# Seven tiles of the first projection as three fp32r products, and five buffers for the modulation chunks of the attention calls

## The reference

```python
cos, sin = axial_rope_tables(ROWS)
xc = ctx
for i in range(DEPTH):
    mod_lat = jax.nn.silu(c) @ w_ada[i] + b_ada[i]
    mod_ctx = jax.nn.silu(c_ctx) @ w_ada[i] + b_ada[i]
    ...
    h = modulate(rmsnorm(x, norm_pre_mix[i]), sh1, sc1)
    hc = modulate(rmsnorm(xc, norm_pre_mix[i]), csh1, csc1)
    p = h @ w_in[i]
    q = apply_axial_rope(p[..., :ATTN_WIDTH].reshape(B, S, N_Q_HEADS, HEAD_DIM), cos, sin)
    k = apply_axial_rope(p[..., kv_lo:kv_lo + KV_WIDTH].reshape(B, S, N_KV_HEADS, HEAD_DIM), cos, sin)
    v = p[..., kv_lo + KV_WIDTH:kv_hi].reshape(B, S, N_KV_HEADS, HEAD_DIM)
    u = p[..., kv_hi:]
    kvc = hc @ w_in[i][:, kv_lo:kv_hi]
    ...
    attn = windowed_gqa_with_context(q, k, v, kc, vc, sink[i])
    four = fourier_mix(u, w_fourier[i])
    mix = jnp.concatenate([attn, four], axis=-1) @ w_out[i]
    x_mid = x + g1 * rmsnorm(mix, norm_post_mix[i])
    ...
    x = x_mid + g2 * rmsnorm(swiglu(hf, w_gate[i], w_up[i], w_down[i]), norm_post_ffn[i])
    # layer 0 only: the context tokens take the same way
```

## Time and profile before

| | us |
|---|---|
| runs of the kernel before | 2437.15, 2430.39, 2429.89 |
| median | 2430.39 |
| the profiled execution, its own time | 2433.61 |
| its span in the profile | 2431.8 |
| PE busy | 2335.6 (96% of the span) |
| DVE busy | 1457.4 (60%) |
| ACT busy | 1031.5 (42%) |
| POOL busy | 299.8 (12%) |
| mean granted clock of TensorE | 0.984 |

### The profile page before, as it was taken

How to read it: one execution, slowest core, us unless ns; L and a number is a source line. 1 busy time by engine, 2 the same in 40 slices (tenths; PEclk the granted TensorE clock), 3 DMA queues, 4 the chain that set the end, 5 groups by cost and what they waited for, 6 DMA issues and landing times.

```text
span 2431.8 us, 47179 instructions
## 1 busy us (share of the span) xinstructions
PE 2335.6 (96%) x19072; PEld 2068.1 (85%) x19072; DVE 1457.4 (60%) x2300; ACT 1031.5 (42%) x1614; POOL 299.8 (12%) x242
## 2 busy tenths in 40 slices
PE   7988999999998899899999999999999999999998
PEld 3856899999975799799998889899899988988997
DVE  1053456666525666676677564766766668555765
ACT  2153544454335433343356434433433455435333
POOL 0000000100000000000006427100000035335000
PEclk8999999999999999999999899999999998999999
DMA  6256554454426555355442214654455332225552
GB/s 276 87 208 243 200 182 175 164 187 176 147 104 243 199 182 187 135 185 187 164 139 105 87 55 142 235 181 181 160 188 189 115 132 81 86 74 196 194 181 104
DMA packets 65655, 392.50 MB, mean 161 GB/s; under 512 B 7280, under 2 KB 7536, under 8 KB 28144
## 3 DMA queue, kind: packets, MB, share of 16 engines
q1 hardware_dynamic: 64224, 383.81, 43.3%
q10 hardware_dynamic: 1008, 5.17, 0.5%
q0 software_dynamic: 288, 1.57, 0.2%
HBM read 389.48 MB, written 1.05 MB: 161 GB/s over the span
## 4 chain that ended last, share of the span: by engine, by line
PE 83%; DVE 6%; issue 4%; POOL 3%; DMA 2%; ACT 2%; SPq 0%; POOLq 0%; DVEq 0%; ACTq 0%
PE ps L2173 19%; PE ps L2175 10%; PE ps L2121 8%; PE ps L2122 8%; PE ps L2123 8%; PE ps L2258 6%; PE ps L2127 4%; PE ps L2132 4%; PE ps L2128 3%; POOL t_lo L637 3%; PE ps L2273 2%; PE ps L2595 2%; PE ps L2736 1%; DMA work<-in_wa 1%; PE ps L2069 1%
## 5 line engine op out<-in xcount | busy, mean ns | idle before, releaser
L2173 PE MATMUL ps<-h_parts,w_hi 128*128 128x512 f32 x2000 | 711.9, 398 | 1.6 <-DVE w_lo L1384 1.6
L2175 PE MATMUL ps<-h_parts,w_lo 128*128 128x256 f32 x2000 | 561.7, 281 | 0.0
L2173 PEld LDWEIGHTS ps<-h_parts,w_hi 128*128 128x128 f32 x2000 | 376.0, 188 | 89.4 <-DVE w_lo L1384 2.4
L2175 PEld LDWEIGHTS ps<-h_parts,w_lo 128*128 128x128 f32 x2000 | 378.0, 189 | 0.0
L1384 DVE TENSOR_TENSOR w_lo<-ring_a,w_hi 128x1024 fp32r<-128x1024 f32 x308 | 362.4, 1217 | 12.7 <-ACT w_hi L731 12.5
L2121 PE MATMUL ps<-hid_hi,d_hi 128*128 128x256 f32 x1232 | 349.0, 283 | 0.0
L2122 PE MATMUL ps<-hid_lo,d_hi 128*128 128x256 f32 x1232 | 348.8, 283 | 0.0
L2123 PE MATMUL ps<-hid_hi,d_lo 128*128 128x256 f32 x1232 | 348.6, 283 | 0.0
L764 ACT ACTIVATE sg<-sg 128x256 f32<-128x256 f32 x130 | 54.4, 419 | 649.0 <-DVE sg L1439 649.0
L731 ACT CAST w_hi<-ring_a 128x1024 fp32r<-128x1024 f32 x308 | 305.7, 1041 | 8.9 <-DMA ring_a<-in_wa 8.9
L1439 DVE TENSOR_REDUCE sg<-ps 128x256 f32<-128x512 f32 x130 | 89.8, 691 | 300.0 <-PE ps L2175 300.0
(11 more groups left out here) (332 smaller groups left out, 3743.9 us busy)
## 6 DMA issues: line engine op xcount, KB each, us to landing
ring_a<-in_wa SPq DMA_DIRECT2D x270, 1024.0 KB, 4.8
ring_d<-in_wd SPq DMA_DIRECT2D x154, 512.0 KB, 5.3
ring_d<-in_wa SPq DMA_DIRECT2D x12, 1024.0 KB, 6.7
work<-in_wa SPq DMA_DIRECT2D x6, 1024.0 KB, 19.8
work<-in_small POOLq DMA_DIRECT2D x2, 768.0 KB, 4.7
work<-in_c ACTq DMA_DIRECT2D x1, 1088.0 KB, 5.0
c<-in_c ACTq DMA_DIRECT2D x1, 1045.0 KB, 7.2
x<-in_x ACTq DMA_DIRECT2D x1, 1024.0 KB, 12.7
```

Of the source, the lines that this page charges most:

```text
L2173: nc.tensor.matmul(out, w_hi[:, f % 2, part, k, :], h_parts[:, k], start=(k == 0), stop=False, skip_group_check=True)
L2175: mm = nc.tensor.matmul(out[:, 1, :], w_lo[:, f % 2, part, k, :], h_hi[:, k, :], start=False, stop=(k == KD - 1), skip_group_check=True)
```

## The change

1. Tiles 2, 3, 4 and 6 to 9 of the first projection are made from hi and lo parts in three fp32r products. Tiles 2 to 4 keep the weights stationary (split_project). Tiles 6/7 and 8/9 are made as pairs: 128 tokens stationary, two weight tiles side by side moving, 256 columns (split_pair); the pairs write four half banks each, banks 6 and 7, then 4 and 5. Tiles 0, 1 and 5 stay fp32.
2. DVE rounds h2 and makes the rests, eight times two of each: latent parts in h_parts, context parts in other_hi and other_lo, which lie in a part of the work area that attention uses later. ACT rounds each of the seven weight tiles (round_first) between its copies, and DVE subtracts. The parts of tiles 2 to 7 lie in t_hi and t_lo, those of 8 and 9 in pair_hi and pair_lo. An odd split tile raises a_used when DVE has its rest, not when PE is done.
3. The modulation chunks go to five buffers in turn: by index modulo 5, two to ring_a, one to ring_d, and two to spares, which is the memory of t_hi and t_lo. For layer 0 the first ring_d chunk and the first ring_a chunk are loaded before, the first two into spares once PE has finished pair 6/7 (proj_ready). A spare buffer is loaded again once the chunk five before has been used (spare_used).

```diff
+        with nc.sbuf_tensor("spares", [P, 2, 2, KD, P], F32) as spares:
+            pass
...
+        OTHER_PARTS, PAIR_HIGH = 7424, 3 * 2 * 2 * KD * P + 2 * 2 * T
+        with ExitStack() as first_parts:
+            first_parts.enter_context(nc.sbuf_tensor("first_gap", [P, OTHER_PARTS], F32))
+            other_hi, other_lo = (first_parts.enter_context(nc.sbuf_tensor(n, [P, KD, T], F32R))
+                                  for n in ("other_hi", "other_lo"))
+            first_parts.enter_context(nc.sbuf_tensor("second_gap", [P, PAIR_HIGH - OTHER_PARTS - 2 * KD * T], F32))
+            pair_hi = first_parts.enter_context(nc.sbuf_tensor("pair_hi", [P, 2, KD, P], F32R))
...
-        in_thirds = {"adaL0": 0, "adaL1": 2 * ADA_STEP0 // 3}
-        thirds = {"adaL0": 2 * ADA_STEP0 // 3, "adaL1": ADA_STEP1 // 3}
+        spares_of = {f"adaL{l}": [i for i in range((2 * ADA_STEP0, ADA_STEP1)[l]) if i % 5 >= 2] for l in range(LAYERS)}
...
+        SPLIT_TILES = [2, 3, 4, 6, 7, 8, 9]
+        first_hi_of = {t: n + 1 for n, t in enumerate(SPLIT_TILES)}
+        first_even_of = {t: n + 1 for n, t in enumerate(t for t in SPLIT_TILES if t % 2 == 0)}
+        def first_weights(t):
+            if t >= 8:
+                return pair_hi[:, t % 2], pair_lo[:, t % 2]
+            return t_hi[:, t % 2], t_lo[:, t % 2]
...
+            def load_spare(name, first, i):
+                n, slot, turn = spare_chunk(ada_from[name[3:]] + i)
+                if i >= 5:
+                    sp.wait_ge(spare_used, n - 2)
+                sp.dma_start(spare_buffers[slot].rearrange("p a b c -> p (a b c)"), wa[first + i])\
+                    .then_inc(spare_loaded[slot], 16)
+            def load_ada(name, first, count):
+                if spare0[name]:
+                    sp.wait_ge(spare_used, spare0[name])
+                load_spare(name, first, 2)
+                if not spare0[name]:
+                    c = ada_chunk(ada_from[name[3:]])
+                    load_a(c, c % 2, wa[first])
+                    sp.wait_ge(proj_ready, first0["proj10"] + 4)
+                for i in (3, 4):
+                    load_spare(name, first, i)
+                for i in range(0 if spare0[name] else 1, count):
+                    if i not in spares_of[name]:
+                        c = ada_chunk(ada_from[name[3:]] + i)
+                        load_a(c, c % 2, wa[first + i])
+                    elif i >= 5:
+                        load_spare(name, first, i)
...
+                def round_first(t):
+                    c = chunk0[stage] + t // 2
+                    if t % 2 == 0:
+                        act.wait_ge(a_loaded[c % 2], 16 * (c // 2 + 1))
+                    nc.scalar.copy(first_weights(t)[0], ring_a[:, c % 2, t % 2]).then_inc(first_round, 1)
+                def empty_pair(t, bank):
+                    act.wait_ge(proj_ready, first0[stage] + t // 2 + 1)
+                    src = ps[:, bank:bank + 2, :].rearrange("p a (b c) -> p (a b) c", c=2 * P)
+                    for u in range(2):
+                        j = t + u - 2 - QT
+                        nc.scalar.copy(u_tok[:, 0:4, j * P:(j + 1) * P], src[:, :, u * P:(u + 1) * P])\
+                            .then_inc(proj_free, 1)
...
                 if l == 0:
+                    round_first(2)
+                    round_first(3)
                     empty_k(0)
-                    for j in range(QT):
-                        empty_q(1 + j, j)
+                    empty_q(1, 0)
+                    empty_q(2, 1)
+                    round_first(4)
+                    act.wait_ge(first_hi, 1)
+                    nc.scalar.copy(raw[:, 3, 0:n_q], ps[:, 4 + (tile0[stage] + 3) % 2, 0:n_q]).then_inc(proj_free, 1)
+                    empty_q(4, 3)
+                    round_first(6)
+                    round_first(7)
                     empty(stage, 1 + QT, v_tok, slice(0, 2 * T))
-                    for j in range(QT):
-                        empty_u(2 + QT + j, j)
+                    round_first(8)
+                    round_first(9)
+                    empty_pair(6, 6)
+                    empty_pair(8, 4)
...
+                    for k in range(KD + 1):
+                        if k < KD - 1:
+                            dve.wait_ge(h2_part, k + 1)
+                        elif k == KD - 1:
+                            dve.wait_ge(norm_out, n_id[second] + 1)
+                        if k < KD:
+                            nc.vector.tensor_copy(h_hi[:, k, :], h2[:, k, 0:T])
+                            nc.vector.tensor_copy(other_hi[:, k, :], h2[:, k, T:2 * T]).then_inc(first_rest, 1)
+                        if k:
+                            dve.wait_ge(first_rest, k)
+                            nc.vector.tensor_tensor(h_lo[:, k - 1, :], h2[:, k - 1, 0:T],
+                                                    h_hi[:, k - 1, :].bitcast(F32), ALU.subtract)
+                            nc.vector.tensor_tensor(other_lo[:, k - 1, :], h2[:, k - 1, T:2 * T],
+                                                    other_hi[:, k - 1, :].bitcast(F32), ALU.subtract).then_inc(first_lo, 1)
+                    for t in SPLIT_TILES:
+                        c = chunk0["proj10"] + t // 2
+                        hi, lo = first_weights(t)
+                        dve.wait_ge(first_round, first_hi_of[t])
+                        if t % 2:
+                            dve.wait_ge(a_used, c)
+                        nc.vector.tensor_tensor(lo, ring_a[:, c % 2, t % 2], hi.bitcast(F32), ALU.subtract)\
+                            .then_inc(a_used if t % 2 else first_even, 1)
...
+            def split_project(t):
+                c, p = chunk0["proj10"] + t // 2, tile0["proj10"] + t
+                w_high, w_low = first_weights(t)
+                out = lambda which: ps[:, 4 + p % 2, which * T:(which + 1) * T]
+                pe.wait_ge(proj_free, p - 1)
+                pe.wait_ge(first_round, first_hi_of[t])
+                for k in range(KD):
+                    if t == SPLIT_TILES[0]:
+                        pe.wait_ge(first_lo, k + 1)
+                    for which, (hi, lo) in enumerate(parts_of):
+                        nc.tensor.matmul(out(which), w_high[:, k, :], hi[:, k, :], start=(k == 0 and which == 0),
+                                         stop=False, skip_group_check=True)
+                        nc.tensor.matmul(out(which), w_high[:, k, :], lo[:, k, :], start=False, stop=False,
+                                         skip_group_check=True)
+                if t % 2:
+                    pe.wait_ge(a_used, c + 1)
+                else:
+                    pe.wait_ge(first_even, first_even_of[t])
+                for k in range(KD):
+                    for which, (hi, _) in enumerate(parts_of):
+                        mm = nc.tensor.matmul(out(which), w_low[:, k, :], hi[:, k, :], start=False,
+                                              stop=(k == KD - 1 and which == 1),
+                                              skip_group_check=True)
+                mm.then_inc(first_hi if t % 2 else proj_ready, 1)
+            def split_pair(t, bank):
+                c = chunk0["proj10"] + t // 2
+                high, low = (t_hi, t_lo) if t < 8 else (pair_hi, pair_lo)
+                def out(b):
+                    return ps[:, bank + b // 2, b % 2 * 2 * P:(b % 2 + 1) * 2 * P].rearrange("p (a c) -> p a c", c=P)
+                def tokens(v, b):
+                    return lambda k: v[:, k, b % 2 * P:(b % 2 + 1) * P]
+                pe.wait_ge(first_round, first_hi_of[t + 1])
+                for b in range(4):
+                    hi, lo = (tokens(v, b) for v in parts_of[b // 2])
+                    for k in range(KD):
+                        nc.tensor.matmul(out(b), hi(k), high[:, :, k, :], start=(k == 0 and b % 2 == 0), stop=False,
+                                         skip_group_check=True)
+                        nc.tensor.matmul(out(b), lo(k), high[:, :, k, :], start=False, stop=False, skip_group_check=True)
+                pe.wait_ge(a_used, c + 1)
+                for b in range(4):
+                    hi = tokens(parts_of[b // 2][0], b)
+                    for k in range(KD):
+                        mm = nc.tensor.matmul(out(b), hi(k), low[:, :, k, :], start=False, stop=(k == KD - 1 and b % 2 == 1),
+                                              skip_group_check=True)
+                mm.then_inc(proj_ready, 1)
...
                     project(stage, 0, h2, slice(0, 2 * T), mixed=(0, 1))
-                    for i in range(1, QT + 1):
-                        project(stage, i, h2, slice(0, n_q))
+                    project(stage, 1, h2, slice(0, n_q))
+                    for t in (2, 3, 4):
+                        split_project(t)
                     project_tokens(stage, QT + 1, h2, 4)
-                    project_tokens(stage, QT + 2, h2, n_q // P)
+                    split_pair(6, 6)
                     turn_heads()
```

(53 more changed lines are left out.)

14 lines of the change are left out of this document (9 added, 5 removed).

## The result

| | median us | lowest to highest | runs |
|---|---|---|---|
| before, all runs on this chip | 2433.80 | 2429.89 to 2437.15 | 5 |
| after | 2419.11 | 2418.45 to 2419.55 | 5 |
| after / before | 0.994 | 0.9927 to 0.9952 (95%) | |

The change makes the kernel 0.6% faster. The profiled execution of after took 2419.11 us with a span of 2417.3 us, 14.5 us under the span of before; the forecast took 14.5 us off. Its 2416 was 3 us low in absolute terms because it was hung on the median of three runs, 2430.39; two more runs moved that median to 2433.80, and from there the change is -14.7 us.

The account below looks back on a forecast made before the run. TensorE was taken to bound the kernel (83% of the chain of waits, the DMA 2%). 2433.61 - 8.5 (projection) - 6.0 (attention call 1) = 2419.1 us, or 2416 from the median of 2430.39; range 2410 to 2424.

Parts of the forecast that it names:

- The price of a product: First projection: each 256-column fp32r product costs 0.1196 us, as in the first feed-forward call.
- the rival of quick products: First projection: products as quick as the lone-product rule, 3.5 us more gain, 2412.5 us; chance 0.05.
- The projection: First projection: seven tiles gain 9.03 us, less 0.5 for the last copies, so the stage ends 8.5 us earlier.
- late weights rival: First projection: weights of tiles 8 and 9 come late, pair 8/9 waits 5.5 us, 2421.5 us; chance 0.05.
- The added 0.5 us of copies: End of the first projection: the second of the last two copies is not hidden and adds 0.5 us.
- The beat of call 1: Attention call 1: without late chunks every head pair takes 3.45 us, saving 3.4 us together.
- The head start: Attention call 1: five of twelve chunks are loaded ahead; the other seven land by 204.2 us, before use at 206.4.
- The DMA's rate: Attention call 1: the DMA is at its limit at 372 GB/s, 2.82 us for a chunk.
- The tail of call 1: End of attention call 1: transposes start 2.4 us sooner, and the stretch to the output projection shrinks by 0.2 us.
- the bound of 7.2: Attention call 1: upper bound on its gain, 5.7 us of waits plus some 1.5 us of half-clock loss; 6.0 taken.
- Only the projection pays: Attention call 1 stays bound by its loads, so only the projection's 8.5 us is gained, 2422 us; chance 0.08.
- Slower: the clock: First projection: fp32r products granted only 1.2 GHz, 0.096 us more each, 32 us in all, 2448 us; chance 0.03.

Follow-up runs that it names:

- h_halves: Changed kernel, each pair making its latent-token products first, then the context ones, ScalarE copying each half when done: 2417.99 us, 0.9934 of before.
- d_no_ahead: Changed kernel with five buffers, but no modulation chunk of attention call 1 issued before the Fourier stage ahead of it is through: 2425.71 us, 0.9966 of before.
- c_four: Changed kernel with four buffers for the modulation chunks in place of five: 2419.05 us, 0.993 of before.
- a_proj_only: Changed kernel with its fp32r projection kept but three modulation chunk buffers in place of five: 2422.33 us, 0.9949 of before.
- b_buffers_only: Changed kernel with its five buffers kept but the projection in fp32 as before: 2426.83 us, 0.9967 of before.
- p_narrow: Changed kernel with pair 6/7 in 192 products of 128 columns in place of 96 of 256: 2427.88 us, 0.9972 of before.

## Why the prediction was right

**The price of a product.** Forecast 0.1196 us, from another stage; the rows of after have 0.12, and tiles 2 to 4 are 5.76 us apart (5.74). The rule of the Trainium skill's page "TensorE: Matmul & The Clock Gate", section "Back-to-back issue gap", gives 109 ns at 256 columns for a product by itself; the 0.12 us of after don't agree, and the rival of quick products falls.

**The projection.** Forecast 8.5, measured 59.73 - 51.25 = 8.48. All of the cover held: VectorE's pieces were ready 2 us earlier than the 47.6 forecast (16 casts and 16 subtractions overlap at their ends, 0.20 and 0.34 us from start to start), the casts of tiles 8 and 9 were in time, and the late weights rival falls. The added 0.5 us of copies came as 0.48 (1.16 - 0.68), and h_halves shows that it could be had back.

**The beat of call 1.** Forecast 3.4 us: from the first pair's maximum to the eighth's, seven beats, before took 27.52 us and after 197.03 - 172.90 = 24.13, 3.39 less. The head start was named as the reason; d_no_ahead shows it.

**The DMA's rate.** Here a size was wrong. The prediction took 372 GB/s and 2.82 us a chunk as the DMA's limit. The earlier trace rows has 420 GB/s at 279 us, before itself moved 425 at 189 to 195 us of call 1, and d_no_ahead 420, 2.50 us a chunk. A chunk sized too long errs on the safe side: no wait was left in after either way. What a chunk takes isn't settled by it: c_four's last chunk was later than 2.82 us apiece gave.

**The tail of call 1.** Here too a term was mis-sized: "2.4 + 0.2" us. From the last probabilities to the output projection before took 217.24 - 211.84 = 5.40 us, after 202.68 - 200.55 = 2.13: 3.27 us less. Both parts were too small by 0.3: the transposes start 0.14 us before the last normalisation's recorded end (200.41 against 200.55), not 0.2 behind it, and from there to the output projection they need 2.27 us where the 2.80 of before were thought to shrink by 0.2. Before was slowed there by its clock of 0.66; a_proj_only, at full clock, puts the clock's share in the whole call at 1.2 us. The whole stretch gave 6.67 against 6.0, within the bound of 7.2; from a_proj_only to after, both at full clock, it is 5.44. Whether the late chunks brought before's clock down isn't shown: b_buffers_only and h_halves have a lowered clock in this call with no wait for a DMA. So 1.2 of the 6.67 us can't be put down to the change for certain.

**The rest.** Call 0 and what lies between kept their time (58.33 against 58.32), and so did everything behind the output projection (2214.62 against 2214.56). Sum of the stages: 8.48 + 6.67 - 0.01 - 0.06, less the 0.57 us by which the start came later, is 14.5 us. That this is the forecast to the tenth is partly luck: 0.67 us too little in call 1 and 0.57 us of a later start, which no term had, cancel. "Only the projection pays" falls with call 1's waits at zero. "Slower: the clock" falls with a granted clock of 1.00 in these windows of after:

```profile
49.81:55.50 5.69, 5.69 (x47) 5.45 (x46) 1.23 (x1) 0.59 (x1) 0.00 (x0) 1.00 0.65 226
55.00:97.00 42.00, 42.00 (x349) 41.74 (x348) 10.49 (x9) 8.26 (x11) 0.00 (x0) 1.00 0.44 174
```

**The absolute number.** Three runs of before were too few to hang a forecast on: 2430.39 was at the low end of a program whose executions spread over 2429 to 2445. The sum against the profiled execution, 2419.1, was the better forecast.

## What to carry to other kernels

Price a split into three fp32r products by their number and their width together: against the fp32 products of this kernel it paid with 256 columns behind each weight load, and by p_narrow's price it would lose at 128. For a stage bound by its loads, count how many chunks can be there when it starts; a further buffer matters through that head start. And where effects are smaller than the spread of executions, compare lengths between the same two events in the profiles, with the granted clock beside them.

## What the runs showed of the hardware

The same two fp32 tiles, with nothing changed in them, took 15.1 us in some executions and 13.57 in others. In before, after (15.11) and h_halves (15.10) the granted clock was 0.50 at 36 to 38 us, in the others 1.00. The windows of after and of d_no_ahead:

```profile
36.00:38.00 2.00, 2.00 (x4) 0.69 (x3) 2.00 (x8) 2.00 (x5) 0.00 (x0) 0.50 0.41 52
```

```profile
36.00:38.00 2.00, 2.00 (x6) 0.79 (x6) 2.00 (x9) 2.00 (x5) 0.00 (x0) 1.00 0.50 78
```

In the same way call 1's stretch has 1.3 us more in h_halves (clock 0.70 at 176 to 180 us) and in b_buffers_only than in after, with no wait to explain it, and the unchanged rest of the program took between 2212.6 and 2219.1 us. What sets this from one execution to the next stays open.

One core's loads reached 420 GB/s over 20 us (d_no_ahead, a DMA share of 1.00), against 372 in the stretch of before that looked saturated at a share of 0.97. Why the two differ stays open.
